# Beginning the first step of a chunked delta-rule scan beside the gates' projection that stands ahead of it

## The chip, the cores and the metric

The kernel runs on one core of one Trainium2 chip. The metric is the device time of one execution in microseconds; the table below gives the median of three runs and the one execution that the hardware profiler recorded.

## What is computed

The reference is two networks one after the other: a hybrid block of two layers, and a second block whose layers are a gated unit, an RWKV-7 layer, a latent attention and again a gated unit. The change lies in the RWKV-7 layer. Its features are projections of the modulated and shifted input `h`, and its scan is a delta rule over 16 heads of 64, once forward and once backward, first over the 256 tokens of the context and then over the 512 of the sequence:

```python
xs = h[:, :, None, :] + xx[:, :, None, :] * mu
rkvz = jnp.einsum('blcd,cde->blce', xs[:, :, :4], w_in)      # r, k, v, z
...
kk = (kk * lax.rsqrt(jnp.sum(kk * kk, axis=-1, keepdims=True) + 1e-12)).reshape(k.shape)
k_dir = k * (1 + (a - 1) * k_a)
...
def step(S, inp):
    s_kk = jnp.einsum('nbhvk,nbhk->nbhv', S, kk_t)
    S = S * w_t[..., None, :] - s_kk[..., :, None] * (kk_t * a_t)[..., None, :] + v_t[..., :, None] * k_t[..., None, :]
    y_t = jnp.einsum('nbhvk,nbhk->nbhv', S, inp[5]) if emit else None
...
return (out * jax.nn.silu(z)) @ w_out
```

The gates `z` are used only in the last line, after the scan.

## The kernel before

One stage of the program follows the other, and for each stage every engine has its own instruction stream, written out by hand: `features_*` makes r, k, v and z, `scan_*` runs the scan, `output_*` closes the layer. SP is the queue that loads, POOL the one that stores in the features. Matrices are kept with channels on the 128 partitions and the 768 tokens (256 + 512) in the columns.

**The features.** `features_pe_` makes four projections in the order r, k, v, z. Each is a wave (`wave_pe`) over m = 0 to 7, eight tiles of 128 output channels, and for each m there is one product of 256 and one of 512 columns (the two segments), of eight matmuls each. A matmul in 32-bit floats is two records in the profile. The products of one m go to PSUM banks 6 and 7, those of the next to 0 and 1, and ACT takes them out; banks 2 to 5 (`side`) are for small work which a wave calls behind each product by `beside(m, lo)`, where `lo` is 0 behind the first segment and 256 behind the second. For m = 0 and 7 the two segments are interleaved (line 1720). In the z wave (`behind_z`) the small work is one transpose of values behind m = 0. ACT puts the tiles through Silu (line 1984), and POOL stores them (line 2176). r, kk, the key products ka and kd and the log decays lw have been stored to device memory during the earlier waves; the scan loads them back tile by tile.

**The scan.** There are 12 steps, each a direction and a tile of 128 tokens, that is two chunks of 64. A step has three parts, each a generator on every engine:

- `chosen(s)`: PE sums the log decays in four pieces (`decays`, L2320, banks 0 to 3), ACT takes the exponentials of each piece (L2521, L2522), DVE multiplies them into kk and ka (L2623, L2626, the events `al` and `be`) and into kd and r. PE then forms the key products `L` (64 by 64 blocks, L333), ACT copies them with a sign (L2531, `nL`), and DVE inverts 16 by 16 blocks of them in a long row of small operations (L2642 to L2719), ACT scales the result (L2536), and DVE turns it (L2667, L2670, the event `out`).
- `solved(s)`: PE completes the inverse by block products (`blocks(0)`, `blocks(1)`, then a series), with masks by DVE (L2752) and POOL (L2846) between, and forms the products with the values.
- `carried(s)`: the state is taken through the two chunks.

`scan_slots` runs slots: in the slot that begins with s, PE and its partners interleave `chosen(s + 2)`, `solved(s + 1)` and `carried(s)` by a string of turns. The first slot (s = -2) therefore holds `chosen(0)` alone, the second (s = -1) `chosen(1)` and `solved(0)`.

**The border.** SP, ACT, DVE and POOL each begin the scan with waits on `ends(pl, "features") + stored(pl)`: on the last event of every engine in the features, and on the landing of every store, the gates' (`S_.z0`, `S_.z1`) among them. PE waits only for its operands. The scan's buffers lie in the arena `A` and over the ring of weight slabs `W` (rows of step 0, 1 and 2 and the keys of even steps in the ring), at addresses which the features' `h`, `xx`, `xs` and the slabs of the z wave use until the end.

Of the kernel before, what the change touches and what calls it, by code (L numbers as in the profile page):

```python
# [16 lines left out]
SC = 256  # L17
# [1852 lines left out]
def features_act(pl, e):  # L1870
# [124 lines left out]
def features_dve(pl, e):  # L1995
# [137 lines left out]
    end(pl, "features", "dve")  # L2133


def features_pool(pl, e):
# [40 lines left out]
    end(pl, "features", "pool")  # L2177


def stored(pl):  # L2180

    S_ = pl.S
    return [S_.lw0.at(10), S_.lw1.at(11), S_.r_out.at(7), S_.kk0_out.at(6), S_.kk1_out.at(7), S_.kd0_out.at(7),
            S_.kd1_out.at(7), S_.ka0_out.at(6), S_.ka0_out1.at(7), S_.ka1_out.at(6), S_.ka1_out1.at(7), S_.vt0.at(6),
            S_.vt1.at(7), S_.bon0.at(6), S_.bon1.at(7), S_.z0.at(6), S_.z1.at(7), S_.res.at("out")]

# [5 lines left out]


def lay_scan(pl):
    ring = pl.W[:, :, :].rearrange("p a b -> p (a b)")
    A, b = Arena(pl, beyond=2 * N), Place()
    b.AR = [ring[:, 2048 * i:2048 * i + 2048].rearrange("p (m a c) -> p m a c", m=8, a=2) for i in range(3)]
    keys = [ring[:, 6144:8192], A(2048)]  # L2200
    b.KA = [x[:, 0:1024].rearrange("p (m c) -> p m c", m=8) for x in keys]
    b.KD = [x[:, 1024:2048].rearrange("p (m c) -> p m c", m=8) for x in keys]
    b.LW, b.E, b.EM = A(1024), A(8, 2, P), A(8, P)
    b.VU = [A(1024) for _ in range(3)]
    b.GT = [A(16, 64) for _ in range(2)]
    b.RK = [[A(16, 64) for _ in range(2)] for _ in range(2)]
    b.KB = [[A(1024) for _ in range(2)] for _ in range(2)]
    b.nL, b.T16, b.Q16 = A(16, 64), A(16, 64), A(16, 64)
    b.nEt, b.nE, b.Z1, b.Z2 = A(16, 64), A(16, 64), A(16, 64), A(16, 64)
    b.Q = [A(16, 64) for _ in range(2)]  # L2210
    b.X, b.HB = A(1024), [A(8, P) for _ in range(2)]
    b.turned = A(1024)
    b.N, b.S = A(272), A(272)
    b.EL, b.EF, b.sc = A(4, 8), A(4, 8), A(8)
    return b


# [27 lines left out]
def scan_slots(pl, e, chosen, solved, carried, order):  # L2245


    for s in range(-2, SCAN_LAST):
        slots({"1": chosen(pl, e, s + 2) if s + 2 < SCAN_LAST else nothing(),
               "2": solved(pl, e, s + 1) if 0 <= s + 1 < SCAN_LAST else nothing(),  # L2250
               "c": carried(pl, e, s) if s >= 0 else nothing()}, order)


def scan_sp(pl, e):
# [11 lines left out]
    def decays(s):  # L2266
        n, tile = SCAN_STEPS[s]
        if s:
            e.wait_ge(*S_.decay_sums.at(s - 1, 3))
        e.dma_start(b.LW, pl.F[f"lw{n}"][tile]).then_inc(*S_.slw.next(s))  # L2270

    def keys(s):
        n, tile = SCAN_STEPS[s]
        if s >= 2:
            e.wait_ge(*S_.gram.at(s - 2, "last"))
        for name, dst, signal in ((f"ka{n}", b.KA[s % 2], (S_.ska0, S_.ska1)[s % 2]),
                                  (f"kd{n}", b.KD[s % 2], (S_.skd0, S_.skd1)[s % 2])):
            e.dma_start(dst, pl.F[name][tile].rearrange("p (m c) -> p m c", m=8)).then_inc(*signal.next(s))

    def rows(s):  # L2280
        n, tile = SCAN_STEPS[s]
        if s >= 3:
            e.wait_ge(*S_.carried.at(2 * (s - 3) + 1, "Y"))
        for name, a, signal in (("kk", 0, (S_.skk0, S_.skk1, S_.skk2)[s % 3]),
                                ("r", 1, (S_.sr0, S_.sr1, S_.sr2)[s % 3])):
            e.dma_start(b.AR[s % 3][:, :, a, :], pl.F[name][tile].rearrange("p (m c) -> p m c", m=8)).then_inc(
                *signal.next(s))

    for s in range(-3, SCAN_LAST):
# [16 lines left out]
    end(pl, "scan", "pe")  # L2306


def chosen_pe(pl, e, s):

    S_, b = pl.S, pl.scan
    n, _ = SCAN_STEPS[s]
    for j in range(4):
        at = ("decays", s, j)
        ps = take(pl, at, "0123")
        if j == 0:
            e.wait_ge(*S_.slw.at(s))
        e.wait_ge(*free(pl, at))
# [282 lines left out]

def scan_dve(pl, e):
    S_, b = pl.S, pl.scan
    for event in ends(pl, "features") + stored(pl):
        e.wait_ge(*event)
    e.memset(b.S, 0.0).then_inc(*S_.dve_wrote.next())
    e.wait_ge(*S_.dve_wrote.last())
    e.memset(b.S[:, 0:272:17], 1.0).then_inc(*S_.dve_wrote.next())
    e.memset(b.N, 0.0).then_inc(*S_.dve_wrote.next())
    e.wait_ge(*S_.dve_wrote.last())  # L2610
# [1263 lines left out]
```

## Time and profile before

| | us |
|---|---|
| median of three runs | 5358.34 |
| the three runs | 5358.34, 5347.9, 5358.88 |
| the profiled execution | 5337.04 |
| its span, first to last instruction | 5335.2 |
| PE busy in the span | 4952.2 |

The profiled execution has 1.84 us around its span, and it is 21.30 us shorter than the median of the runs. PE is busy in 93% of the span, DVE in 28% and ACT in 20%, so what matters is where PE has nothing to do. The border between the features and the scan lies at about 3097 us of the span.

### The profile page before, as it was taken

Reading aid. Unit: us, or ns where it says so; the run is one execution under the profiler, and the core shown is the slowest. Engines: PE = TensorE matmul, PEld = TensorE weight load, DVE = VectorE, ACT = ScalarE, POOL = GpSimd, SP = SyncE. Lnnn points to the kernel's source line nnn. Section 1 sums busy time; section 2 is a strip of 40 time slices with the busy share of each in tenths; the row PEclk is TensorE's granted clock in tenths of the full one; section 3 lists DMA queues with packets and bytes.
Section 4 is the critical chain, followed back from the end, with each engine's and each line's share of the span. In section 5 each row is a group of like instructions: output and inputs, shape, how many; then the busy total and the mean of one; then the engine's idle time right before and its main releaser. Section 6 shows DMA issues by size and latency. Waiting matters only on the chain.

```text
span 5335.2 us, 63185 instructions
## 1 busy us (share of the span) xinstructions
PE 4952.2 (93%) x27502; PEld 2753.1 (52%) x27502; DVE 1480.8 (28%) x2779; ACT 1074.7 (20%) x2066; POOL 323.9 (6%) x302
## 2 busy tenths in 40 slices
PE   7878999987899999999998978988899999989999
PEld 3444444444444444665454557877544555544444
DVE  1272120227222010110324146665311344410100
ACT  1121000012200012110214123433211333311210
POOL 0110000011000000000014100000000011000000
PEclk9879999987999999999999989999999999989999
DMA  3232212213212211111134222121311000101211
GB/s 114 84 123 78 79 67 75 73 72 126 87 71 74 71 53 63 49 52 41 63 128 134 102 84 72 52 71 28 119 54 53 22 26 27 41 25 70 87 71 55
DMA packets 91874, 378.39 MB, mean 71 GB/s; under 512 B 8144, under 2 KB 33744, under 8 KB 62160
## 3 DMA queue, kind: packets, MB, share of 16 engines
q1 hardware_dynamic: 78048, 327.44, 17.2%
q0 software_dynamic: 9808, 37.75, 2.1%
q10 hardware_dynamic: 3744, 9.14, 0.5%
q8 instruction: 220, 3.60, 0.3%
q14 instruction: 54, 0.44, 0.0%
HBM read 334.46 MB, written 39.85 MB: 70 GB/s over the span
## 4 chain that ended last, share of the span: by engine, by line
PE 69%; DVE 4%; ACT 2%; issue 2%; DMA 0%; POOL 0%; POOLq 0%; DVEq 0%; ACTq 0%; SPq 0%
PE ps L521 29%; PE ps L333 20%; PE ps L542 5%; PE ps L3265 2%; PE ps L1720 1%; PE ps L3192 1%; PE ps L339 1%; PE ps L3276 1%; PE ps L2370 1%; PE ps L3195 1%; PE ps L3191 1%; PE ps L921 1%; PE ps L3193 1%; PE ps L2320 0%; PE ps L1751 0%
## 5 line engine op out<-in xcount | busy, mean ns | idle before, releaser
L521 PE MATMUL ps<-A,W 128*128 128x512 f32 (+1 forms) x5408 | 2167.3, 561 | 23.4 <-DVE A L1643 6.2
L521 PEld LDWEIGHTS ps<-A,W 128*128 128x128 f32 x5408 | 1028.1, 191 | 1119.6 <-issue 1076.8
L333 PE MATMUL ps<-A,W 128*128 128x512 f32 (+3 forms) x2368 | 665.1, 445 | 13.7 <-DMA W<-in_rw_in 6.0
L333 PE MATMUL ps<-A 64*64 64x64 f32 (+3 forms) x8416 | 511.1, 242 | 114.1 <-ACT A L3418 23.1
L333 PEld LDWEIGHTS ps<-A 64*64 64x64 f32 (+2 forms) x8416 | 471.0, 153 | 223.5 <-issue 142.3
L333 PEld LDWEIGHTS ps<-A,W 128*128 128x128 f32 (+2 forms) x2368 | 352.9, 174 | 303.9 <-issue 273.3
L542 PE MATMUL ps<-W,A 128*128 128x512 f32 (+1 forms) x896 | 366.1, 572 | 1.8 <-ACT A L1507 1.8
L542 PEld LDWEIGHTS ps<-W,A 128*128 128x128 f32 x896 | 173.2, 194 | 192.9 <-issue 186.5
L435 ACT ACTIVATE A<-R 128x512 f32<-128x512 f32 (+1 forms) x96 | 52.6, 574 | 779.7 <-DVE R L1517 354.9
L1637 DVE SCALAR_TENSOR_TENSOR A<-ps,V,A 128x512 f32<-128x512 f32 (+1 forms) x48 | 31.0, 661 | 486.9 <-PE ps L333 486.3
L1517 DVE SCALAR_TENSOR_TENSOR R<-ps,MOD,R 128x512 f32<-128x512 f32 (+1 forms) x48 | 31.7, 662 | 439.8 <-PE ps L521 438.5
L339 PE MATMUL ps<-C,A 128*128 128x128 f32 x608 | 102.5, 295 | 46.6 <-DVE A L1187 46.4
L3409 ACT ACTIVATE A<-ps,A 128x256 f32<-128x256 f32 (+1 forms) x128 | 84.8, 667 | 293.9 <-DVE A L3530 293.9
L333 PE MATMUL ps<-W,A 64*64 64x64 f32 (+3 forms) x1856 | 137.7, 255 | 4.6 <-ACT A L2550 2.8
L1653 POOL TENSOR_TENSOR A<-A 128x1536 f32<-128x1536 f32 (+1 forms) x16 | 46.4, 2900 | 1526.6 <-ACT A L1610 1526.6
L339 PEld LDWEIGHTS ps<-C,A 128*128 128x128 f32 x608 | 71.7, 146 | 123.5 <-DVE A L1187 65.0
L333 PEld LDWEIGHTS ps<-W,A 64*64 64x64 f32 (+1 forms) x1856 | 119.6, 160 | 27.0 <-issue 22.2
L1610 ACT ACTIVATE A<-ps 128x256 f32<-128x256 f32 (+1 forms) x96 | 50.3, 526 | 369.9 <-PE ps L521 369.7
L1451 DVE TENSOR_TENSOR A<-A,ps 128x512 f32<-128x512 f32 x44 | 30.3, 689 | 334.0 <-PE ps L521 334.0
L3528 DVE TENSOR_REDUCE A<-ps 128x1 f32<-128x256 f32 (+1 forms) x128 | 71.4, 558 | 138.6 <-PE ps L3193 138.1
L1418 ACT ACTIVATE A<-ps 128x512 f32<-128x512 f32 x44 | 26.3, 597 | 369.3 <-PE ps L521 369.3
L2550 ACT ACTIVATE A<-ps 64x512 f32<-64x512 f32 x144 | 85.2, 591 | 62.2 <-PE ps L333 60.2
(353 smaller groups left out, 4238.1 us busy)
## 6 DMA issues: line engine op xcount, KB each, us to landing
W<-in_ada SPq DMA_DIRECT2D x48, 1024.0 KB, 5.4
W<-in_w_up SPq DMA_DIRECT2D x44, 1024.0 KB, 4.8
W<-in_w_down SPq DMA_DIRECT2D x32, 704.0 KB, 4.0
W<-in_w_in SPq DMA_DIRECT2D x18, 1024.0 KB, 4.8
W<-in_sgu_v SPq DMA_DIRECT2D x16, 1024.0 KB, 4.8
W<-in_sgu_u SPq DMA_DIRECT2D x16, 1024.0 KB, 4.7
W<-in_sgu_z SPq DMA_DIRECT2D x16, 1024.0 KB, 4.8
W<-in_sgu_o SPq DMA_DIRECT2D x16, 1024.0 KB, 4.8
```

The source lines that it names most:

```text
L333: r = e.matmul(out, a, b, start=start and i == 0, stop=stop and i == len(pairs) - 1, skip_group_check=loose)
L339: return e.transpose(out, in_, table(pl, "ident")[0:k, 0:k])
L521: t = e.matmul(ps, w[:, k, c:c + mc], x(k, seg), start=k == 0, stop=k == kt - 1)
L542: mm = e.matmul(ps, x(k0 + k, tile), w[:, k, :], start=k0 + k == 0, stop=k0 + k == kt - 1)
L921: t = e.matmul(ps[32 * k:32 * k + 32, :], b.cs[:, 4 * hf + k, :], w[:, k, :], start=hf == 0, stop=hf == 1)
L1720: t = e.matmul(y, w[:, k, :], b.x(k, s), start=k == 0, stop=k == 7)
L2370: e.matmul(by_heads(ps[c][HALF[c], :]), one[HALF[c], :], i, start=True, stop=False, skip_group_check=True)
L2550: e.activation(dst[HALF[c], 8 * g:8 * g + 8, :], by_heads(bank(pl, at)[HALF[c], :]), ACT.Copy).then_inc(*S_.act_blocks.next((s, g, stage), ...
L3191: e.matmul(ps[0][:, 0:SC], qn, kh[:, 0:SC], start=True, stop=False)
L3265: t = e.matmul(ps[:, :], uq[j][:, k, 0:P], b.cq[:, k, :], start=k == 0, stop=k == 5)
L3409: e.activation(b.pr[:, z, lo:hi], bank(pl, at)[:, 0:hi - lo], ACT.Exp, bias=m[:, 2:3], scale=b.rq[:, p % 2, 2 * i + j:2 * i + j + 1], accu ...
L3528: e.tensor_reduce(m[:, part:part + 1], bank(pl, at)[:, 0:w], AX, ALU.max).then_inc(*made.next())
```

## The change

The first step's `chosen(0)` is taken out of the scan and given to the features, beside the z wave, and the scan begins with the slot s = -1. The buffers are laid anew so that everything that `chosen(0)` touches lies in the first 11,880 columns of the arena, where only `h` and `xx` were, which the last interpolation of the z wave (`lerped.at(3, 7)`) is the last to read; what lay in the ring for step 0 is in the arena, and the masked products `GT` are in the ring. SP loads step 0 and the decays of step 1 behind the z wave's slabs. At the start of the scan POOL waits for all stores as before; SP, ACT and DVE no longer wait for those of the gates.

```diff
@@ features_sp @@
             slab_load(pl, e, ("rw_in", c, m), ins["rw_in"][c, m])
+    first_step_sp(pl, e)
@@ features_pe_ @@
+    first = chosen_pe(pl, e, 0, side)
+
     def behind_z(m, lo):
         if m == 0 and not lo:
             turn(7)
+        for _ in range({1: 4, 2: 1}.get(m, 0) if lo else 0):
+            next(first)
@@ features_act @@
+    first = chosen_act(pl, e, 0)
     for m in range(8):
         for s in segs:
...
                 *S_.act_projected.next(at, frees=at))
+            for _ in range({(1, SC): 4, (3, 0): 1, (5, 0): 1}.get((m, s[0]), 0)):
+                next(first)
@@ features_dve @@
+    first_step_dve(pl, e)
     end(pl, "features", "dve")
+
+
+def first_step_dve(pl, e):
+    S_, x = pl.S, pl.scan
+    e.wait_ge(*S_.lerped.last())
+    for event in keys_stored(pl):
+        e.wait_ge(*event)
+    e.memset(x.S, 0.0).then_inc(*S_.dve_wrote.next())
...
+    for _ in chosen_dve(pl, e, 0):
+        pass
@@ lay_scan @@
-    b.AR = [ring[:, 2048 * i:2048 * i + 2048].rearrange("p (m a c) -> p m a c", m=8, a=2) for i in range(3)]
-    keys = [ring[:, 6144:8192], A(2048)]
+    rows = [A(2048), ring[:, 0:2048], ring[:, 2048:4096]]
+    keys = [A(2048), ring[:, 4096:6144]]
+    b.AR = [x.rearrange("p (m a c) -> p m a c", m=8, a=2) for x in rows]
...
+    b.GT = [ring[:, 6144 + 1024 * i:7168 + 1024 * i].rearrange("p (h c) -> p h c", h=16) for i in range(2)]
@@ scan_slots @@
-    for s in range(-2, SCAN_LAST):
+    for s in range(-1, SCAN_LAST):
@@ new @@
+def first_step_sp(pl, e):
+
+    e.wait_ge(*pl.S.lerped.at(3, 7))
+    for event in keys_stored(pl):
+        e.wait_ge(*event)
+    decays_sp(pl, e, 0)
+    keys_sp(pl, e, 0)
+    rows_sp(pl, e, 0)
+    decays_sp(pl, e, 1)
@@ scan_sp @@
-    for event in ends(pl, "features") + stored(pl):
+    for event in ends(pl, "features") + keys_stored(pl) + values_stored(pl):
@@ chosen_pe @@
-        ps = take(pl, at, "0123")
+        ps = take(pl, at, ring)
@@ scan_act, scan_dve @@
-    for event in ends(pl, "features") + stored(pl):
+    for event in ends(pl, "features") + values_stored(pl):
@@ scan_pool @@
-    for event in ends(pl, "features") + stored(pl):
+    for event in ends(pl, "features") + keys_stored(pl) + values_stored(pl) + [S_.z0.at(6), S_.z1.at(7)]:
```

The order on PE at the border, before: behind the last pair of the z wave (L1720) come the four pieces of step 0's decays (L2320), the key products of step 0, two pieces of step 1's decays, and then `blocks(0)` of step 0. A matmul is one row here.

```order
L1720 MATMUL ps1<-A,W 128x512
L2320 MATMUL ps0<-C,A 128x256 [waits act_projected,slw]
...
L2320 MATMUL ps3<-C,A 128x256 [waits value_copied]
L2320 MATMUL ps3<-C,A 128x256
L333 MATMUL ps0<-W 64x64 [waits decayed,dve_operands]
L333 MATMUL ps1<-W 64x64
...
L2320 MATMUL ps2<-C,A 128x256 [waits decayed,slw]
L2320 MATMUL ps2<-C,A 128x256
L2320 MATMUL ps3<-C,A 128x256 [waits decayed]
L2320 MATMUL ps3<-C,A 128x256
L333 MATMUL ps0<-A 64x64 [waits act_blocks,decayed,blocks_solved]
```

PE has this whole row of work between its last z product and `blocks(0)`. The same engine and place of the changed kernel, where the decays have line 2368:

```order
L1721 MATMUL ps1<-A,W 128x512
L2368 MATMUL ps0<-C,A 128x256 [waits act_projected,slw]
L2368 MATMUL ps0<-C,A 128x256
L2368 MATMUL ps1<-C,A 128x256 [waits act_projected]
L2368 MATMUL ps1<-C,A 128x256
L333 MATMUL ps2<-A 64x64 [waits act_blocks,decayed,blocks_solved]
```

Step 0's pieces and key products are gone from here, and step 1's two pieces are now in banks 0 and 1, which the last tiles of the z wave hold until ACT has taken them out. `blocks(0)` takes banks 2, 3, 0 and 1.

In the z wave of the changed kernel, PE behind m = 1 and m = 2:

```order
L333 MATMUL ps1<-A,W 128x512 x7
L2368 MATMUL ps2<-C,A 128x256 [waits value_copied,slw]
...
L2368 MATMUL ps5<-C,A 128x256 [waits value_copied]
L2368 MATMUL ps5<-C,A 128x256
L333 MATMUL ps6<-A,W 128x256 [waits act_projected,slab0]
L333 MATMUL ps6<-A,W 128x256 x7
L333 MATMUL ps7<-A,W 128x512 [waits act_projected]
L333 MATMUL ps7<-A,W 128x512 x7
L333 MATMUL ps2<-A 64x64 [waits decayed,dve_operands]
```

The eight matmuls of the decays stand between m = 1 and m = 2, and the 32 of the key products, of which the last row is the first, between m = 2 and m = 3; before, these products followed one another with nothing between.

On ACT in the changed kernel the exponentials stand between the tiles of m = 1 and m = 2:

```order
L2569 ACT_TABLE_LOAD
L2569 ACTIVATE A<-ps2 128x512 [waits decay_sums]
L2570 ACTIVATE A<-ps2 128x256
L2569 ACTIVATE A<-ps3 128x512 [waits decay_sums]
L2570 ACTIVATE A<-ps3 128x256
...
L1990 ACT_TABLE_LOAD [waits z0]
L1990 ACTIVATE A<-ps6 128x256 [waits projected]
```

There are two table loads more than before on ACT, both here, and the one at the start of the scan stays.

## Rows read from the trace of the kernel before

**Rows 1.** The page: span, and busy time of each engine.
```profile
span 5335.2 us, 63185 instructions
PE 4952.2 (93%) x27502; PEld 2753.1 (52%) x27502; DVE 1480.8 (28%) x2779; ACT 1074.7 (20%) x2066; POOL 323.9 (6%) x302
```

**Rows 2.** Chain of work from 3013 to 3140 us: start, us, what.
```profile
3024.81 61.96 PE ps L333 x192
...
3098.29 2.59 DMA g_z<-A
...
3101.02 3.62 DMA A<-f_lw
...
3117.01 1.98 DVE A L2642 x2
...
3131.58 1.76 DVE A L2667 x2
```

**Rows 3.** PE in order of time, 3084 to 3165 us: start, us, instructions, idle before.
```profile
3086.59 10.49 PE L1720 MATMUL ps<-A,W 128*128 128x256 f32 x32
3104.69 5.98 PE L2320 MATMUL ps<-C,A 128*128 128x256 f32 x16 [7.61 <-DMA A<-f_lw]
3113.85 1.98 PE L333 MATMUL ps<-W 64*64 64x64 f32 x64 [3.19 <-DVE A L2627]
...
3133.43 3.52 PE L333 MATMUL ps<-A 64*64 64x64 f32 x64 [13.88 <-DVE A L2667]
3137.72 1.99 PE L2320 MATMUL ps<-C,A 128*128 128x256 f32 x8 [0.78 <-DVE A L2752]
3140.77 2.10 PE L333 MATMUL ps<-A 64*64 64x64 f32 x64 [1.05 <-ACT A L2522]
...
3150.01 1.10 PE L333 MATMUL ps<-A,W 64*64 64x64 f32 x62
```

**Rows 4.** Windows: length, busy time and count by engine, PEclk, DMA share, GB/s.
```profile
3013.00:3097.00 84.00, 83.42 (x262) 48.93 (x262) 8.93 (x11) 7.09 (x15) 5.84 (x10) 1.00 0.15 58
3112.00:3133.00 21.00, 5.69 (x72) 4.35 (x72) 17.80 (x33) 4.30 (x10) 0.00 (x0) 0.60 0.46 135
3137.00:3165.00 28.00, 19.14 (x452) 15.46 (x453) 21.63 (x40) 11.72 (x23) 2.19 (x2) 0.98 0.09 30
3165.00:3640.00 475.00, 426.04 (x9135) 377.10 (x9134) 306.40 (x509) 183.10 (x350) 19.62 (x18) 0.96 0.23 66
```

**Rows 5.** ACT in order of time, 3097 to 3112 us.
```profile
3097.12 0.87 ACT L1984 ACTIVATE A<-ps 128x256 f32<-128x256 f32 x2 [9.73 <-PE ps L1720]
3106.87 1.28 ACT L2521 ACT_TABLE_LOAD   x1 [8.88 <-PE ps L2320]
3108.16 0.60 ACT L2521 ACTIVATE A<-ps 128x512 f32<-128x512 f32 x1
...
3109.39 0.41 ACT L2522 ACTIVATE A<-ps 128x256 f32<-128x256 f32 x1
```

**Rows 6.** DVE in order of time, 3111 to 3147 us.
```profile
3112.53 1.22 DVE L2626 TENSOR_TENSOR W<-W,A 128x1024 f32<-128x1024 f32 x1
...
3136.98 2.85 DVE L2752 TENSOR_TENSOR A<-ps,C 64x512 f32<-64x512 f32 x4 [3.66 <-PE ps L333]
3142.91 2.85 DVE L2752 TENSOR_TENSOR A<-ps,C 64x512 f32<-64x512 f32 x4 [3.07 <-PE ps L333]
3145.79 1.23 DVE L2623 TENSOR_TENSOR W<-W,A 128x1024 f32<-128x1024 f32 x1
```

**Rows 7.** POOL in order of time, 3095 to 3150 us.
```profile
3101.10 1.84 POOL L2830 MEMSET A<- 128x1024 f32 x2 [2.27 <-DMA g_z<-A]
3138.48 1.09 POOL L2846 TENSOR_TENSOR A<-A,C 128x512 f32<-128x512 f32 x1 [35.54 <-DVE A L2752]
```

**Rows 8.** DMA issues, 3095 to 3130 us: count, KB each, us from issue to landing.
```profile
W<-f_kk SPq DMA_DIRECT2D x2, 512.0 KB, 7.2
W<-f_r SPq DMA_DIRECT2D x2, 512.0 KB, 8.8
```

More of the change, by code:

```diff
@@ L2132, in features_dve @@
                 *S_.value_copied.next((m, s[0]), frees=at))
+    first_step_dve(pl, e)
     end(pl, "features", "dve")
+def first_step_dve(pl, e):
[4 more added lines that the diff above has]
+    e.memset(x.S, 0.0).then_inc(*S_.dve_wrote.next())
+    e.wait_ge(*S_.dve_wrote.last())
+    e.memset(x.S[:, 0:272:17], 1.0).then_inc(*S_.dve_wrote.next())
+    e.memset(x.N, 0.0).then_inc(*S_.dve_wrote.next())
+    e.wait_ge(*S_.dve_wrote.last())
+    for _ in chosen_dve(pl, e, 0):
+        pass
 def features_pool(pl, e):
@@ L2177, in features_pool, with keys_stored, values_stored @@
     end(pl, "features", "pool")
-def stored(pl):
+def keys_stored(pl):
     S_ = pl.S
     return [S_.lw0.at(10), S_.lw1.at(11), S_.r_out.at(7), S_.kk0_out.at(6), S_.kk1_out.at(7), S_.kd0_out.at(7),
-            S_.kd1_out.at(7), S_.ka0_out.at(6), S_.ka0_out1.at(7), S_.ka1_out.at(6), S_.ka1_out1.at(7), S_.vt0.at(6),
-            S_.vt1.at(7), S_.bon0.at(6), S_.bon1.at(7), S_.z0.at(6), S_.z1.at(7), S_.res.at("out")]
+            S_.kd1_out.at(7), S_.ka0_out.at(6), S_.ka0_out1.at(7), S_.ka1_out.at(6), S_.ka1_out1.at(7)]
+def values_stored(pl):
+    S_ = pl.S
+    return [S_.vt0.at(6), S_.vt1.at(7), S_.bon0.at(6), S_.bon1.at(7), S_.res.at("out")]
 SCAN_ORDER = ([0, 1, 2, 3, 4, 5], [1, 0, 5, 4, 3, 2])
@@ L2198, in lay_scan @@
     A, b = Arena(pl, beyond=2 * N), Place()
-    b.AR = [ring[:, 2048 * i:2048 * i + 2048].rearrange("p (m a c) -> p m a c", m=8, a=2) for i in range(3)]
-    keys = [ring[:, 6144:8192], A(2048)]
+    rows = [A(2048), ring[:, 0:2048], ring[:, 2048:4096]]
+    keys = [A(2048), ring[:, 4096:6144]]
+    b.AR = [x.rearrange("p (m a c) -> p m a c", m=8, a=2) for x in rows]
     b.KA = [x[:, 0:1024].rearrange("p (m c) -> p m c", m=8) for x in keys]
     b.KD = [x[:, 1024:2048].rearrange("p (m c) -> p m c", m=8) for x in keys]
+    b.GT = [ring[:, 6144 + 1024 * i:7168 + 1024 * i].rearrange("p (h c) -> p h c", h=16) for i in range(2)]
     b.LW, b.E, b.EM = A(1024), A(8, 2, P), A(8, P)
+    b.nL, b.T16, b.Q16 = A(16, 64), A(16, 64), A(16, 64)
+    b.N, b.S = A(272), A(272)
+    b.EL, b.EF, b.sc = A(4, 8), A(4, 8), A(8)
     b.VU = [A(1024) for _ in range(3)]
-    b.GT = [A(16, 64) for _ in range(2)]
     b.RK = [[A(16, 64) for _ in range(2)] for _ in range(2)]
-    b.KB = [[A(1024) for _ in range(2)] for _ in range(2)]
-    b.nL, b.T16, b.Q16 = A(16, 64), A(16, 64), A(16, 64)
-    b.nEt, b.nE, b.Z1, b.Z2 = A(16, 64), A(16, 64), A(16, 64), A(16, 64)
     b.Q = [A(16, 64) for _ in range(2)]
     b.X, b.HB = A(1024), [A(8, P) for _ in range(2)]
+    b.KB = [[A(1024) for _ in range(2)] for _ in range(2)]
     b.turned = A(1024)
-    b.N, b.S = A(272), A(272)
-    b.EL, b.EF, b.sc = A(4, 8), A(4, 8), A(8)
+    b.nEt, b.nE, b.Z1, b.Z2 = A(16, 64), A(16, 64), A(16, 64), A(16, 64)
     return b
@@ L2251, in scan_slots, with decays_sp, keys_sp, rows_sp @@
                "c": carried(pl, e, s) if s >= 0 else nothing()}, order)
+def decays_sp(pl, e, s):
+    S_, b = pl.S, pl.scan
+    n, tile = SCAN_STEPS[s]
+    if s:
+        e.wait_ge(*S_.decay_sums.at(s - 1, 3))
+    e.dma_start(b.LW, pl.F[f"lw{n}"][tile]).then_inc(*S_.slw.next(s))
+def keys_sp(pl, e, s):
+    S_, b = pl.S, pl.scan
+    n, tile = SCAN_STEPS[s]
+    if s >= 2:
+        e.wait_ge(*S_.gram.at(s - 2, "last"))
+    for name, dst, signal in ((f"ka{n}", b.KA[s % 2], (S_.ska0, S_.ska1)[s % 2]),
+                              (f"kd{n}", b.KD[s % 2], (S_.skd0, S_.skd1)[s % 2])):
+        e.dma_start(dst, pl.F[name][tile].rearrange("p (m c) -> p m c", m=8)).then_inc(*signal.next(s))
+def rows_sp(pl, e, s):
+    S_, b = pl.S, pl.scan
+    n, tile = SCAN_STEPS[s]
+    if s >= 3:
+        e.wait_ge(*S_.carried.at(2 * (s - 3) + 1, "Y"))
+    for name, a, signal in (("kk", 0, (S_.skk0, S_.skk1, S_.skk2)[s % 3]),
+                            ("r", 1, (S_.sr0, S_.sr1, S_.sr2)[s % 3])):
+        e.dma_start(b.AR[s % 3][:, :, a, :], pl.F[name][tile].rearrange("p (m c) -> p m c", m=8)).then_inc(
+            *signal.next(s))
+def first_step_sp(pl, e):
[6 more added lines that the diff above has]
+    decays_sp(pl, e, 1)
 def scan_sp(pl, e):
     S_, b = pl.S, pl.scan
-    for event in ends(pl, "features") + stored(pl):
+    for event in ends(pl, "features") + keys_stored(pl) + values_stored(pl):
         e.wait_ge(*event)
@@ L2264, in values @@
             *(S_.sv0, S_.sv1, S_.sv2)[u % 3].next(u))
[L2266 to L2289, printed above, removed]
+    for s in range(-2, SCAN_LAST):
         if 0 <= s + 1 < SCAN_LAST:
             values(2 * s + 2)
-        if s + 3 < SCAN_LAST:
-            decays(s + 3)
+        if 1 < s + 3 < SCAN_LAST:
+            decays_sp(pl, e, s + 3)
         if 0 <= s + 1 < SCAN_LAST:
@@ L2296, in scan_sp @@
         if s + 3 < SCAN_LAST:
-            keys(s + 3)
-            rows(s + 3)
+            keys_sp(pl, e, s + 3)
+            rows_sp(pl, e, s + 3)
 def scan_pe(pl, e):
@@ L2306, in scan_pe, with chosen_pe @@
     end(pl, "scan", "pe")
-def chosen_pe(pl, e, s):
+def chosen_pe(pl, e, s, ring="0123"):
     S_, b = pl.S, pl.scan
@@ L2324, in chosen_pe @@
     at = [("L", s, par) for par in range(2)]
-    ps = [take(pl, x, "0123") for x in at]
+    ps = [take(pl, x, ring) for x in at]
     e.wait_ge(*S_.dve_operands.at(s, "al"))
@@ L2603, in scan_dve @@
     S_, b = pl.S, pl.scan
-    for event in ends(pl, "features") + stored(pl):
+    for event in ends(pl, "features") + values_stored(pl):
         e.wait_ge(*event)
[L2606 to L2610, printed above, removed]
     scan_slots(pl, e, chosen_dve, solved_dve, carried_dve, "2 2 1 1 c 1 1 1 1 1 1 1 2 1 2 2 c".replace(" ", ""))
@@ L2826, in scan_pool @@
     S_, b = pl.S, pl.scan
-    for event in ends(pl, "features") + stored(pl):
+    for event in ends(pl, "features") + keys_stored(pl) + values_stored(pl) + [S_.z0.at(6), S_.z1.at(7)]:
         e.wait_ge(*event)
```

## The prediction

> **What bounds the kernel now.** I read the page first: PE is busy in 4952.2 of 5335.2 us [rows 1], so a change of this kind can win only where PE stands idle or slow. The chain of waits shows the place. It runs through PE's z wave up to 3097.08 us (3086.59 + 10.49 [rows 3]), and then leaves PE: the store of the last gates lands (2.59 us), the log decays of step 0 are loaded (3.62), PE sums them, ACT and DVE work, PE makes the key products, and from 3117.01 to 3133.34 it is nearly all DVE, with ACT once between [rows 2]. Only at 3133.43 does PE begin `blocks(0)` of step 0, after 13.88 us in which it waited for DVE [rows 3]. From the last z product to `blocks(0)` are 36.35 us, and PE has work in about 11.7 of them (5.98 + 1.98 + two pieces of step 1's decays, which hide in the gap). The windows show the second loss: the granted clock, 1.00 during the z wave, averages 0.60 from 3112 to 3133 and is 0.98 in the slot after [rows 4]; it is the lower of the two levels, 1.2 GHz, for most of the gap, which PE entered after 7.61 us without work [rows 3].
>
> **What the change removes.** Everything between 3097.08 and 3133.43 goes from the path: the wait for the last gates' store, the load of the decays, step 0's sums and exponentials, its operands, the key products, and the 16.3 us of inverse blocks. These are run beside the z wave, where DVE, after its last interpolations and value copies, and ACT are nearly idle: 8.93 and 7.09 us of 84 [rows 4].
>
> **What it puts into the z wave.** PE is the bound there (83.42 of 84 us, and the six tiles m = 1 to 6 follow one another in 61.96, 10.33 each [rows 2, 4]), so all its added work counts in full.
> - The decays of step 0 are 16 records of 128x256. At full clock 8 of them take 1.99 us with their tail [rows 3], so 3.98 is the upper bound; the z wave's own pace gives the lower: 61.96 us over 96 records of 256 and 96 of 512 columns is 0.215 for a 256, or 3.44. I take 3.7.
> - The key products are 64 records of 64x64. Step 1's, at full clock, are 62 in 1.10 and two more just before [rows 3]; I take 1.2. The 1.98 at 3113.85 was at the low clock and is the upper end.
> - Sum 4.9 (4.6 to 6.0); the z wave ends at 3102.0.
>
> Does PE wait in the wave? Behind m = 1 (about 3035.0, that is 3024.8 + 10.3) the sums take 3.7. ACT takes a table load of 1.28 and four pairs of exponentials, two of which took 1.64 (3108.16 to 3109.80 [rows 5]), and is through by about 3041; DVE's `al` and `be`, 1.2 each [rows 6], are ready by 3043.5. PE comes to the key products at 3038.7 + 10.3 = 3049.0: 5.5 us of cover. If that cover were gone, each us late would stop the z products queued behind. The loads of step 0 are issued at about 3020, when the last interpolation is done, and even the slowest landing, 8.8 us for r [rows 8], is in before its use. ACT's two added table loads (2.6 us) delay Silu tiles, but a bank is wanted again only two tiles, 20 us, later. DVE's inverse (16.3 us from 3055) ends by 3080, the scaling on ACT behind m = 5 included, 20 us before it is needed. SP stands in the wait for step 0's sums, with only step 1's decays behind it; POOL issues the gates' stores as before. All of this I cost at nothing.
>
> **What stays on the path behind the wave.** `blocks(0)` needs four banks, and two of them now hold step 1's pieces, which before were made and taken out in the gap. So, from 3102.0: ACT takes the tile out of bank 0 and PE begins the first piece, 0.6 us (the two tiles took 0.87 [rows 5]); four records at 0.23 and the hand-over to ACT, 1.3 (before, at half clock, 2.18 from 3104.69 to 3106.87 [rows 3, 5]); the table load 1.28; two pairs of exponentials 1.64; and back to PE 0.15. `blocks(0)` begins at 3102.0 + 5.0 = 3107.0, against 3133.43: **26.4 us** earlier.
>
> It also begins at full clock. Before, DVE could begin the first mask 3.55 us after its start (3136.98), while for `blocks(1)`, the same 64 products at full clock, it was 2.14 (3140.77 to 3142.91) [rows 3, 6]. That gives **1.4 us** more if PE keeps its clock over about 3.5 us with little work.
>
> The ScalarE: Activation LUTs page of the Trainium skill (What ACT_TABLE_LOAD costs) speaks against part of this: a switch to another set costs about 1.28 us and a drain of about 1.38, and one switch stands on the path. The trace shows the next activation at 3108.16, right after the load's 1.28 us [rows 5], with no drain behind it; by the page's price the gain would be 1.4 us less than by my sum.
>
> **Does something else come late?** SP issues the keys and rows of step 1 only after ACT's last z tile, at about 3103.1, where before they were on their way 22 us ahead of `blocks(0)`. Four issues take about 2 us, and the slowest landing 8.8 [rows 8], so they are in by 3114. DVE wants kk of step 1 12.36 us after `blocks(0)` began (3145.79 [rows 3, 6]), less 1.4 for the clock: at 3118.0. The cover is 4 us, and thin. POOL still waits for the last gates' store: 3103.2 + 2.6, then the two memsets of 1.84 [rows 7], by 3108; its first add is wanted 1.5 us behind the first mask (3138.48 against 3136.98 [rows 6, 7]), at 3110.6. The rest of the scan (3165 to 3640, PE 426 of 475 us [rows 4]) has the same order with buffers at other addresses and banks turned by two; nothing in it starts at a fixed time, so it shifts as a whole.
>
> **Sum.** 26.4 + 1.4 = 27.8 us, bounds 22 (blocks at low clock, dearer inserted work, the exponentials late by 2) to 30 (inserted work at its lower bound, no wait for bank 0). Span 5335.2 - 27.8 = 5307.4, and with the 1.8 us around it the profiled execution would be 5309.2. The median of the runs shown is 21.3 us above the profiled execution; against it the forecast is 5358.34 - 27.8 = 5330.5. Between a profile at 5337.04 and runs up to 5358.88 some 10 us either way come from the runs, not from the change. What a measurement of this kernel can tell from no change is about 0.2%, 10.7 us.
>
> **Rivals.**
> - *The clock falls in the slot after* (chance 0.09). PE is busy in only 19.14 of 28 us there [rows 4], and the scan as a whole ran at 0.96. For: the clock did fall after the 7.61 us idle. Against: before, this slot kept 0.98. Half of its 19 us of work at half speed costs 10: 5340.
> - *Step 1's rows, or the operands in the wave, come late* (0.05). It decides once four transfers need more than 4 us beyond the slowest seen. At 10 us of wait the time is 5340.
> - *The change doesn't bring forward what ends the scan* (0.04): a later slot waits for something that starts when it did before, and gives the gain back. I find no such wait in the rows; 5358.
> - *Slower* (0.04). A wave that PE ran without a gap gets two short pieces of other work, one of them 64x64 products. If the clock fell there and did not come back until the wave's end, the five tiles behind, 51.6 us, would take twice as long: 5330.5 + 51.6 = 5382. It turns the result once the low clock holds for 28 us. Against: the z wave, transposes and all, shows 1.00 [rows 4], and the added work leaves no idle time.
>
> **How the numbers follow.** The forecast has 0.78, with a range of its own of 5318 to 5342 (the bounds of the sum and the scatter of the runs). The first two rivals lie at its upper end. I give 5314 to 5346, which leaves out the last two and the tails. Faster by over 0.2%: 0.78 + 0.09 + most of 0.05, 0.91; within 0.2%: 0.05; slower: 0.04.
>
> **What the changed profile should show.** PE has no wait above 0.5 us in the z wave, which ends 4.6 to 6.0 us later. The granted clock is 1.00 across the border. A table load on ACT stands right behind the first piece of step 1. `blocks(0)` starts 9.5 to 11 us behind the old end of the wave and takes 2.1 us, not 3.5. DVE's long row of small operations lies between 3055 and 3080. After that each slot is as long as it was. I am wrong if PE waits for the key products' operands, if DVE in the slot after waits for kk of step 1, or if the clock falls.

## The result: 0.67% faster by the first runs, 0.34% by all of them

| | kernel before | changed kernel |
|---|---|---|
| first session, median (5 runs each) | 5358.34 | 5316.88 |
| ratio there, 95% interval | | 0.9933, 0.9917 to 0.995 |
| profiled execution | 5337.04 | 5318.4 |
| its span | 5335.2 | 5316.6 |
| all runs of all sessions: mean (count) | 5344.5 (88) | 5326.2 (29) |

Over all runs the difference of the means is 18.4 us with a standard error of 2.7; single runs of the kernel before lie between 5319 and 5373 us. The first session's medians of five lay 13.8 us above and 9.3 us below these means, so its difference of 41.5 us is 23 us too large. I therefore read the change where it acts, in the traces. In the rows, `[1.80 <-DVE ...]` means that the engine stood idle for 1.80 us, until DVE had finished. I cut each span in three: the **head**, up to the start of the z wave's first product; the **border**, from there to DVE's first mask of step 0; the **tail**, the rest.

PE of the changed kernel, in order of time from 3005 to 3160 us, answers to [rows 3]:

```profile
3022.13 10.57 PE L1721 MATMUL ps<-A,W 128*128 128x256 f32 x32 [1.80 <-DVE A L2054]
...
3043.52 3.61 PE L2368 MATMUL ps<-C,A 128*128 128x256 f32 x16
3046.97 10.48 PE L333 MATMUL ps<-A,W 128*128 128x256 f32 x32
3057.39 1.16 PE L333 MATMUL ps<-A 64*64 64x64 f32 x64
...
3099.88 10.49 PE L1721 MATMUL ps<-A,W 128*128 128x256 f32 x32
3110.94 1.97 PE L2368 MATMUL ps<-C,A 128*128 128x256 f32 x8 [0.56 <-ACT A L1990]
3115.37 2.10 PE L333 MATMUL ps<-A 64*64 64x64 f32 x64 [2.47 <-ACT A L2570]
3118.35 1.99 PE L2368 MATMUL ps<-C,A 128*128 128x256 f32 x8 [0.88 <-DVE A L2795]
```

Step 0's sums (3.61) and key products (1.16) stand in the wave with no wait; the wave takes 88.24 us (3022.13 to 3110.37), against 83.50 before (3013.58 to 3097.08). `blocks(0)` starts 5.00 us behind it and takes 2.10, at full clock. The start of the wave is 8.55 us later than before, though nothing ahead of it was changed; other runs of both kernels put it elsewhere again (table below).

ACT and DVE of the same kernel, in order of time; they answer to [rows 5] and [rows 6]:

```profile
3112.30 1.28 ACT L2569 ACT_TABLE_LOAD   x1 [1.01 <-PE ps L2368]
3113.59 0.60 ACT L2569 ACTIVATE A<-ps 128x512 f32<-128x512 f32 x1
```

```profile
3048.61 1.23 DVE L2666 TENSOR_TENSOR A<-A 128x1024 f32<-128x1024 f32 x1 [13.80 <-ACT A L2569]
3049.75 1.22 DVE L2669 TENSOR_TENSOR A<-A 128x1024 f32<-128x1024 f32 x1
...
3063.63 1.97 DVE L2685 STREAM_TRANSPOSE A<-A 128x512 f32<-128x512 f32 x2 [10.25 <-ACT A L2579]
...
3086.66 1.90 DVE L2710 STREAM_TRANSPOSE A<-A 128x512 f32<-128x512 f32 x2
3117.61 2.85 DVE L2795 TENSOR_TENSOR A<-ps,C 64x512 f32<-64x512 f32 x4 [29.06 <-PE ps L333]
```

The key products' operands are ready at 3050.97, 6.4 us before PE wants them; the inverse lies between 3063 and 3089, beside the wave. The first mask is at 3117.61: the border is 95.48 us, before 3136.98 - 3013.58 = 123.40. **The border gained 27.9 us.** The tails are 2198.2 us before and 2199.0 after, and with the head's 8.55 that is the difference of the two spans, 18.6.

The windows around it (columns as in [rows 4], the granted clock third from the end) show the clock kept from the wave's end through `blocks(0)`:

```profile
3110.40:3115.40 5.00, 1.99 (x10) 1.49 (x11) 0.00 (x0) 3.79 (x7) 0.54 (x1) 1.00 0.54 172
3115.40:3145.00 29.60, 20.61 (x504) 16.77 (x504) 21.36 (x39) 11.11 (x22) 4.01 (x4) 0.95 0.33 93
```

What the second window lacks is lost at the slot's end: the clock is 1.00 up to 3139, and 0.73 from 3139 to 3145, where PE waits 4.58 us for ACT's scaling. The kernel before has the same wait (4.57).

### The profile page after: what moved, and what is told of

Same layout as the page of the kernel before. It is cut to its first block, busy times and chain, and to the rows that moved or that the text cites. A ratio compares the mean times of both kernels' runs of the same rounds, so it can differ in the third digit from the quotient of the medians.

```text
span 5316.6 us, 63186 instructions
## 1 busy us (share of the span) xinstructions
PE 4958.3 (93%) x27502; PEld 2757.2 (52%) x27502; DVE 1480.1 (28%) x2779; ACT 1077.2 (20%) x2068; POOL 323.9 (6%) x302
## 4 chain that ended last, share of the span: by engine, by line
PE 70%; DVE 4%; ACT 2%; issue 2%; DMA 0%; POOL 0%; POOLq 0%; DVEq 0%; ACTq 0%
PE ps L521 29%; PE ps L333 20%; PE ps L542 5%; PE ps L3308 2%; PE ps L1721 2%; PE ps L3235 1%; PE ps L339 1%; PE ps L3319 1%; PE ps L2418 1%; PE ps L3238 1%; PE ps L3234 1%; PE ps L921 1%; PE ps L3236 1%; PE ps L1752 0%; PE ps L2977 0%
## 5 line engine op out<-in xcount | busy, mean ns | idle before, releaser
L333 PE MATMUL ps<-A,W 64*64 64x64 f32 (+3 forms) x3264 | 711.1, 386 | 44.7 <-DVE R L2859 13.5
L333 PEld LDWEIGHTS ps<-A,W 128*128 128x128 f32 (+2 forms) x3264 | 397.6, 167 | 338.7 <-issue 308.9
L333 PE MATMUL ps<-A 64*64 64x64 f32 (+3 forms) x8416 | 498.7, 243 | 72.6 <-ACT A L3461 23.1
L333 PEld LDWEIGHTS ps<-A 64*64 64x64 f32 (+2 forms) x8416 | 458.0, 153 | 179.3 <-issue 96.3
L333 PE MATMUL ps<-W,A 64*64 64x64 f32 (+3 forms) x1472 | 118.6, 261 | 2.1 <-ACT A L2598 1.9
L333 PEld LDWEIGHTS ps<-W,A 64*64 64x64 f32 (+1 forms) x1472 | 102.5, 164 | 22.6 <-issue 17.9
L2795 DVE TENSOR_TENSOR A<-ps,C 64x512 f32<-64x512 f32 x96 | 66.1, 689 | 136.0 <-PE ps L333 133.7
```

The lines of the kernel that those rows point to most:

```text
L333: r = e.matmul(out, a, b, start=start and i == 0, stop=stop and i == len(pairs) - 1, skip_group_check=loose)
L2795: e.tensor_tensor(dst[HALF[c], 8 * g:8 * g + 8, :], by_heads(bank(pl, at)[HALF[c], :]), masked_by(pl, mask, HALF[c], 8), ALU.mult).then_in ...
```

## The experiments

All parts in us, each row from one profiled execution; x4_early, x5_zwaits, x8_filler and x10_early_filled were executed only this once, and nothing is read from their whole time. *Release* is when PE starts after ACT's scaling of step 1, counted from the start of the z wave; the tail begins at the first mask.

| kernel | head | z wave | border | release | tail |
|---|---|---|---|---|---|
| before | 3013.6 | 83.50 | 123.40 | 150.8 | 2198.2 |
| x11_before | 3010.0 | 83.49 | 122.71 | 150.1 | 2195.3 |
| changed | 3022.1 | 88.24 | 95.48 | 122.9 | 2199.0 |
| x0_again | 3040.1 | 88.24 | 95.48 | 122.9 | 2209.3 |
| x12_third | 3032.0 | 88.25 | 95.48 | 122.9 | 2202.3 |
| x1_waits | 3013.1 | 83.49 | 119.78 | 147.2 | 2202.1 |
| x2_loads | 3031.5 | 83.49 | 115.33 | 142.8 | 2202.8 |
| x3_sums | 3039.3 | 86.95 | 109.96 | 137.4 | 2211.9 |
| x4_early | 3016.0 | 94.63 | 101.87 | 129.3 | 2199.2 |
| x5_zwaits | 3031.5 | 88.24 | 99.08 | 126.5 | 2209.3 |
| x7_next | 3016.1 | 91.69 | 95.20 | 125.8 | 2209.1 |
| x9_filled | 3031.6 | 91.69 | 95.20 | 121.8 | 2199.1 |
| x10_early_filled | 3013.5 | 92.25 | 99.49 | 126.9 | 2201.8 |
| x8_filler | 3028.0 | 83.50 | 122.54 | 150.0 | 2202.4 |

The border of the changed kernel repeats (95.48 three times), that of the kernel before to 0.7 us (123.40 and 122.71). Heads, the same code in all, move by 30 us, and tails, nearly the same code, by 17.

### The same kernels again: x0_again, x11_before, x12_third

No edit.

> The changed kernel once more. I split each profile in three: the head up to the first product of the z wave (before 3013.6 us, changed 3022.1), the border from there to DVE's first mask of step 0 (before 123.4, changed 95.5), and the tail from there to the end of the span (before 2198.2, changed 2199.0). Theory path: the change is worth the border's 27.9 us and nothing else; head and tail vary from run to run with the granted clock, in both kernels. Then the border is 95.5 within 0.3 again, the tail is within 8 us of 2199, and the medians of the two kernels lie 20 to 36 us apart. Rival, more than the border: the medians differed by 41.5 us because the slots after run better as well; then the tail comes out shorter than 2190, or the medians are again 40 us apart.

> The changed kernel a third time, to settle what the runs of the first two left open: its medians were 41.5 us below the kernel before in one session and 8.6 in the other, with single runs scattered over 37 us, while the border measured 95.48 us both times. Theory path: border 95.5 again, head and tail anywhere in 3013 to 3040 and 2198 to 2212; set against the mean granted clock of each run, the two kernels' runs lie on two parallel lines, about 17 us apart at equal clock (the kernel before has some 12 us of clock loss in its own border, which this comparison hides). Rival: the change has a cost in the rest of the program; then the lines are not parallel or lie less than 12 us apart.

> The kernel before, unchanged, as a kernel of its own. Theory path: border 123.4 within 0.3; its head is anywhere in 3013 to 3040 us like that of the changed kernel, so that the 3013.6 of the first profile was one draw; its median differs from that of the other runs of the same kernel by up to 10 us for no reason in the code. Rival: head and tail of the kernel before are shorter than those of the changed one as a rule: head under 3018 again.

Ratios to the kernel before: x0_again 0.9974 (0.9954 to 0.9995), x12_third 0.9959 (0.994 to 0.9978), x11_before 0.9988 (0.9968 to 1.0007). The borders of the changed kernel came as expected. That of x11_before, 122.71, lies 0.7 below the first and missed "within 0.3": behind the same wait of 3.19 us its key products ran at full clock, in 1.16 us, where the first profile has 1.98 [rows 3]. Its head, 3010.0, is under 3018 again, which was the rival's sign; x8_filler, the kernel before with fillers behind this place, has 3028.0, and x1_waits, x4_early and x10_early_filled, with the changed layout, have 3013 to 3016. So a low head is no mark of the kernel before. The medians of x0_again, only 8.6 us apart, missed "20 to 36", and its tail missed "within 8 us" by 2. Each run lists its mean granted clock, and against it both kernels lie on lines: 4.12 us for each 0.001 of clock before (83 runs), 4.28 after (29), with 2.0 and 2.3 us left over. At a clock of 0.953 they stand at 5343.3 and 5325.3, parallel within the scatter and 18.0 us apart, as x12_third's expectation had it (17). So nearly all scatter of the runs goes with the granted clock.

### The change in steps: x1_waits, x2_loads, x3_sums

x1_waits, against the changed kernel (x2_loads leaves `first_step_sp` in the features):

```diff
@@ features_sp, features_pe_, features_act, features_dve @@
-    first_step_sp(pl, e)
...
-        for _ in range({1: 4, 2: 1}.get(m, 0) if lo else 0):
-            next(first)
...
-    first_step_dve(pl, e)
@@ scan_slots, scan_sp, scan_dve @@
-    for s in range(-1, SCAN_LAST):
+    for s in range(-2, SCAN_LAST):
...
+    first_step_sp(pl, e)
...
+    first_step_dve(pl, e)
```

> The changed kernel's layout and its fewer waits, with all work and loads of step 0 back at the start of the scan. Theory path: SP no longer waits for the landing of the last gates (3.0 us), all else is as before: border 123.4 - 3.0 = 120.4 (119.9 to 121.0). Rival, that fewer waits alone make much of the gain: border under 115.

> As x1_waits, with the loads of step 0 issued during the z wave as in the changed kernel; its work still stands in the scan. Theory path: PE begins the sums 0.6 us behind the z wave, where before it was 7.6; its idle is then too short for the clock to fall, which gives 0.9 on the first sum and 0.8 on the key products; blocks(0) still starts at the low clock behind DVE's inverse. Border 123.4 - 7.0 - 1.7 = 114.7 (114 to 117).

x3_sums keeps the sums and what follows from them in the wave:

```diff
-        for _ in range({1: 4, 2: 1}.get(m, 0) if lo else 0):
+        for _ in range({1: 4}.get(m, 0) if lo else 0):
...
```

> As the changed kernel, but only the sums, exponentials and operands of step 0 stand beside the z wave; key products and inverse are in the scan. Theory path: the z wave is 3.6 us longer, then 1.4 for the key products, 1.1 for their copy, 16.4 for the inverse, and 3.5 for a slow blocks(0): border 83.5 + 3.6 + 18.9 + 3.5 = 109.5 (108.5 to 111). The inverse's 16 us on DVE would then be the larger half of the whole gain. Rival, that PE's work in the wave is dearer than its busy time: z wave longer than 88 us.

Borders of 119.78, 115.33 and 109.96 against 120.4, 114.7 and 109.5. Fewer waits gave 3.6 us, early loads 4.5, sums and exponentials beside the wave 5.4, key products and inverse 14.5. Against x11_before the first step is 2.9 us, and 3.0 were expected. x1_waits fell 0.1 below its stated span because the clock was back when the key products came; PE there, in order of time:

```profile
3101.68 5.41 PE L2358 MATMUL ps<-C,A 128*128 128x256 f32 x16 [5.12 <-DMA A<-f_lw]
3110.38 1.16 PE L333 MATMUL ps<-A 64*64 64x64 f32 x64 [3.30 <-DVE A L2661]
```

Their 1.16 us stands against 1.98 in [rows 3], in the kernel before at the low clock. x2_loads is within its span, but not by the way expected: its sums did run at full clock, its key products, behind a longer wait, did not. PE of x2_loads, in order of time:

```profile
3115.55 3.69 PE L2358 MATMUL ps<-C,A 128*128 128x256 f32 x16 [0.56 <-ACT A L1985]
3123.50 1.99 PE L333 MATMUL ps<-A 64*64 64x64 f32 x64 [4.25 <-DVE A L2661]
```

As whole-kernel medians the steps are invisible: 5353, 5340 and 5353 against 5342.6. Set against the clock as above they show: moved along the line to a clock of 0.953, the means of the ten runs each are 5341.7, 5336.3 and 5333.4, in order between 5343.3 and 5325.3. These differences are smaller than the border's, because a comparison at equal clock leaves out what a change gains in clock.

### The waits put back: x5_zwaits

```diff
@@ scan_act, scan_dve; the same two waits are added in scan_sp @@
-    for event in ends(pl, "features") + values_stored(pl):
+    for event in ends(pl, "features") + values_stored(pl) + [pl.S.z0.at(6), pl.S.z1.at(7)]:
```

> The changed kernel with SP's, ACT's and DVE's waits for the gates' stores put back. Theory path: the last store lands some 3 to 5.6 us after its issue at 3111.6 in the changed profile, and ACT may take the first exponential of step 1 only then, not at 3112.3: blocks(0) and the border 2.3 to 5 us later, 98 to 100.5. Rival: these waits are hidden behind PE's first two sums, border 95.5 to 96.

The border is 99.08: 3.6 us dearer, as expected. `blocks(0)` starts 2.2 us later, and the longer wait costs the clock too, another 1.4. PE of x5_zwaits, in order of time:

```profile
3120.26 1.97 PE L2368 MATMUL ps<-C,A 128*128 128x256 f32 x8 [0.56 <-ACT A L1990]
3126.89 3.51 PE L333 MATMUL ps<-A 64*64 64x64 f32 x64 [4.66 <-ACT A L2570]
```

### The cover in the wave: x4_early and x10_early_filled

```diff
-        for _ in range({1: 4, 2: 1}.get(m, 0) if lo else 0):
+        for _ in range({1: 5}.get(m, 0) if lo else 0):
             next(first)
```

> The changed kernel with the key products of step 0 directly behind the sums, ahead of the z products of m = 2. Theory path: PE reaches them at the sums' end, but al and be are ready only 3.9 us later (in the changed profile the sums end at 3047.1 and be at 3050.97), and all z products queue behind: z wave 88.2 + 3.9 = 92.1 us, border 99.4 (98.8 to 100.2). This prices the cover that the chosen place gives. Rival, the clock: an idle PE of 4 us inside the wave brings the low clock and the next products run at half pace; z wave over 94 us.

x10_early_filled puts eight products between:

```diff
+            filler(pl, e, 6, 8)
             next(first)
...
+def filler(pl, e, bank_no, n):
+    e.wait_ge(*pl.bank_freed.get(pl.occupant[bank_no], pl.S.const.last()))
+    for _ in range(n):
+        e.matmul(pl.banks[bank_no][:, 0:256], table(pl, "ident"), pl.C[:, 0:256], start=True, stop=True)
```

> As x4_early, with eight products of 128x256 on constants into a free bank ahead of the key products, in the 3.94 us in which PE waited for their operands. Theory path: x4_early's z wave of 94.6 us was 88.2 + 3.9 of wait + 2.5 of low clock; with the fillers the clock stays, and the wave takes 92.1 (91.9 to 92.4). Rival, that the 2.5 us were something else than the clock: 94.6 again.

x4_early's wave took 94.63 us: the wait is the expected 3.94, and 2.45 more went to the clock. Over 94 us was the rival's sign. Windows of x4_early, columns as in [rows 4]; PEclk is the third number from the end:

```profile
3041.00:3043.00 2.00, 0.02 (x1) 0.00 (x0) 0.50 (x1) 1.98 (x6) 0.00 (x0) 1.00 0.49 104
3043.00:3045.00 2.00, 0.04 (x4) 0.07 (x5) 2.00 (x5) 0.98 (x1) 0.00 (x0) 0.56 0.41 162
3047.00:3049.00 2.00, 2.00 (x5) 1.64 (x6) 0.27 (x1) 0.00 (x0) 0.00 (x0) 0.50 0.00 0
3049.00:3051.00 2.00, 2.00 (x8) 1.62 (x8) 0.00 (x0) 0.00 (x0) 0.00 (x0) 0.74 0.00 0
```

With the fillers PE waited 0.49 us and the wave took 92.25, as the clock reading demands (PE of x10_early_filled):

```profile
3038.34 3.62 PE L2278 MATMUL ps<-C 128*128 128x256 f32 x16
3042.44 1.16 PE L333 MATMUL ps<-A 64*64 64x64 f32 x64 [0.49 <-DVE A L2679]
```

### Step 1's sums in the wave too: x7_next and x9_filled

`begun_pe` is `chosen_pe(pl, e, 1, side)`, and ACT has the same; the slot s = -1 passes over the four turns that this takes from it.

```diff
+        if m == 4 and lo:
+            for _ in range(4):
+                next(pl.begun_pe)
...
@@ scan_pool @@
...
+    for _ in solved_pool(pl, e, 0):
+        pass
+    for event in [S_.z0.at(6), S_.z1.at(7)]:
+        e.wait_ge(*event)
```

> The changed kernel with all four sums and exponentials of step 1 in the z wave too, behind m = 4, and POOL making its first two adds before it waits for the gates' stores. Theory path: the z wave is 3.6 us longer; blocks(0) follows it after 1.0 us (two tiles to take out) and not 5.0; blocks(1) no longer waits for exponentials, 0.9. Border to the first mask 95.5 + 3.6 - 4.0 = 95.1, and 1.3 us in all by the second group of masks (5.9 us behind the first in the changed kernel, 5.0 here). Rival: ACT's two further table loads or PE's added work make the wave longer than that and nothing is won; border 96.5 or more.

x9_filled adds, behind `blocks(0)` of step 0, `filler(pl, e, 7, 6)`.

> As x7_next, with six products of 128x256 columns on constants into a free bank between step 0's first and second block products, whose result nobody uses. In x7_next PE idled 3.1 us there and the clock was at its lower level for the next 10 us: the second masks came 101.5 us behind the start of the z wave (changed kernel 101.4), and PE's first product behind step 1's scaling 125.8 (changed kernel 122.9). Theory path: the fillers keep the clock; first mask 95.2, second 100.3 (100.0 to 100.6), step 1's scaling released at 121 (120 to 122), so 1 to 3 us better than the changed kernel. Rival: what is late in x7_next is not PE's pace but the order; 125 to 126 again.

x7_next: first mask 95.20 as computed, but the second masks at 101.48, where 100.1 was expected, and the release 2.9 us later than in the changed kernel. The runs' median was 5322.55 against 5340.09, ratio 0.9974 (0.9954 to 0.9995). PE idled in the slot, and its products ran slowly. PE of x7_next, in order of time:

```profile
3109.05 2.10 PE L333 MATMUL ps<-A 64*64 64x64 f32 x64 [1.27 <-ACT A L1995]
3114.28 3.24 PE L333 MATMUL ps<-A 64*64 64x64 f32 x64 [3.13 <-DVE A L2809]
3119.11 3.68 PE L333 MATMUL ps<-C,A 128*64 128x128 f32 x32 [1.59 <-DVE A L2809]
```

The same places of x9_filled, with the fillers in the idle time:

```profile
3126.59 2.86 PE L2283 MATMUL ps<-C 128*128 128x256 f32 x12
3129.78 2.10 PE L333 MATMUL ps<-A 64*64 64x64 f32 x64 [0.34 <-DVE A L2817]
3133.48 1.97 PE L333 MATMUL ps<-C,A 128*64 128x128 f32 x32 [1.59 <-DVE A L2817]
```

Second masks at 100.33, release at 121.8: 1.1 us better than the changed kernel and 4.0 better than x7_next, which differs only by useless products. By release x9_filled is the best version made here: median 5315.66 (6 runs) against 5344.72 for the kernel before in its session, ratio 0.994 (0.992 to 0.996). That it beats the changed kernel rests on its trace; 1.1 us does not show in medians.

### A filler in the kernel before: x8_filler

```diff
+    if s == 0:
+        e.wait_ge(*pl.bank_freed.get(pl.occupant[5], pl.S.const.last()))
+        for i in range(26):
+            e.matmul(pl.banks[5][:, 0:256], table(pl, "ident"), pl.C[:, 0:256],
+                     start=True, stop=True)
```

> The kernel before, with 26 products of 128x256 columns on constants into a free bank, on PE ahead of step 0's first block products; nobody uses their result. They keep PE busy while DVE inverts. Theory path: the clock is back at full when blocks(0) starts, so the first mask comes 2.2 us behind its start and not 3.55: border 123.4 - 1.4 = 122.0 (121.8 to 122.3, or 122.5 if the fillers end late). Rival: the slow blocks(0) is not a matter of the clock but of the first use after a wait; border stays 123.4.

Inconclusive. The fillers took 11.4 us and ended 4.54 us early; `blocks(0)` still took 3.46. PE of x8_filler, in order of time:

```profile
3131.12 11.38 PE L2349 MATMUL ps<-C 128*128 128x256 f32 x52
3147.05 3.46 PE L333 MATMUL ps<-A 64*64 64x64 f32 x64 [4.54 <-DVE A L2673]
```

The border of 122.54 is that of x11_before (122.71), whose key products also ran at full clock; the fillers themselves gave at most 0.2 us. x9_filled and x10_early_filled decided the question.

## Why the prediction was right, and what it left out

**The path.** The bound (36.35 us from the wave's end to `blocks(0)`) was read rightly, and the steps x1 to x3 show that it came off in the parts named: waits, loads, exponentials, and as the largest part key products and inverse.

**The inserted work.** Estimated 4.9 us, measured 4.74 (3.61 + 1.16, less what overlaps).

**Behind the wave.** Estimated 5.0 us from its end to `blocks(0)`, measured 5.00. The table load took 1.28 us and the exponential followed 0.01 later. The page ScalarE: Activation LUTs of the Trainium skill (What ACT_TABLE_LOAD costs) has a drain of 1.38 us besides; this trace doesn't show one on the path.

**The clock.** Estimated 1.4 us; `blocks(0)` now leads to its first mask in 2.24 us, not 3.55, so 1.3. The rival that the clock falls in the next slot did not come true here (1.00 up to 3139), but it did in x7_next and x5_zwaits, at 1.4 to 4 us: right as a mechanism, and near.

**Late arrivals.** DVE took up kk of step 1 104.3 us behind the wave's start, as estimated (104.4), 6.8 us after its landing. POOL was mis-sized: I had its memsets done 2.6 us before its first add is wanted. The last gates' store now lands beside step 1's loads, 5.5 us after its issue and not 2.6, and the cover is 0.03 us. POOL of the changed kernel, which answers to [rows 7]:

```profile
3111.57 0.54 POOL L2199 DMA_DIRECT2D g_z<-A  x1 [10.07 <-ACT A L1990]
3117.24 1.84 POOL L2873 MEMSET A<- 128x1024 f32 x2 [5.12 <-DMA g_z<-A]
3119.11 1.08 POOL L2889 TENSOR_TENSOR A<-A,C 128x512 f32<-128x512 f32 x1
```

**The sum.** 27.8 us foreseen, 27.9 in the border (27.2 against x11_before). The bounds of 22 and 30 are wider than the terms named for them, which come to 23.3 and 28.7; and the rival *Slower* counted 28 us of low clock where it needs 28 us of full-clock work at half pace, some 56 us by the clock.

**What was luck.** The measured 5316.88 is inside the stated range, but 13.6 us below the forecast of 5330.5 and 1.1 below the forecast's own range of 5318 to 5342. The first session's 41.5 us owe as much to which five runs were drawn as to the change: over all runs the gain is 18.4 us, and that is 9.4 below the sum and below its lower bound of 22. So the mechanism of the border was right, and one term was not: that everything behind it "shifts as a whole", at no cost.

**What the sum lacked, and what stays open.** The mean over all runs moved by 18.4 us (13 to 24), not 27.9. From the windows, the kernel before loses 0.33 of 36.3 us and 0.06 of 31.0 to the low clock in its border, 13.8 us; the changed kernel 0.05 of 29.6, 1.5. That should raise the mean clock of a run by 12.3 / 5335 = 0.0023, to 0.9551. It is 0.9528 in both. At 4.12 us for 0.001 those 0.0023 are 9.5 us, just what is missing: outside the border the changed kernel's runs had less clock, by more than chance easily gives (the standard errors of the two mean clocks are 0.0003 and 0.0006). One place is seen. A stretch that ends the latent attention, between two table loads of ACT (4634.53 and 4858.62 us in the kernel before), takes 224.1 us in the kernel before, x11_before and x8_filler, 227.9 in the changed kernel's first trace, and 231.5 to 232.2 in the ten others. In both kernels the clock dips and comes back in its first 45 us; it then stays up to 72 us behind the stretch's start in the kernel before, but falls again at 48 in x12_third. The same 60 us of it, from 19 us behind its start, in the kernel before and then in x12_third, windows of 20:

```profile
4653.38:4673.38 20.00, 16.23 (x94) 11.78 (x91) 11.18 (x27) 5.37 (x15) 0.00 (x0) 0.91 0.31 128
4673.38:4693.38 20.00, 13.58 (x68) 8.69 (x68) 6.48 (x18) 5.73 (x16) 0.00 (x0) 0.91 0.00 1
4693.38:4713.38 20.00, 13.50 (x64) 7.60 (x62) 6.64 (x17) 5.59 (x16) 0.00 (x0) 0.91 0.00 0
```

```profile
4640.70:4660.70 20.00, 16.21 (x94) 11.87 (x91) 11.18 (x27) 5.39 (x15) 0.00 (x0) 0.91 0.30 125
4660.70:4680.70 20.00, 14.06 (x52) 8.61 (x52) 5.53 (x16) 5.30 (x16) 0.00 (x0) 0.74 0.00 0
4680.70:4700.70 20.00, 15.42 (x52) 9.77 (x52) 4.96 (x13) 3.94 (x12) 0.00 (x0) 0.66 0.01 1
```

The code there is the same. PE waits 2.5 us for each group of exponentials, in both kernels and at both levels of the clock, and a group takes 7.3 us at the full clock and 10.2 at the low one. Added up in windows of 3 us, the stretch loses 18.2 us to the low clock in the kernel before, x11_before and x8_filler, 20.5 in the changed kernel's first trace, and 25.6 in x0_again, x12_third, x1_waits and x5_zwaits. The 7.4 us between are just what the stretch takes longer; they are most of the missing 9.5, and 0.0014 of the missing 0.0023 in the mean clock of a run. The three traces of the old layout and the eleven of the new part cleanly here. x1_waits is among the eleven, with no work of step 0 in the wave, and so is x5_zwaits, with the waits put back: it needs neither the early work nor the dropped waits. What the eleven share is the new layout of the buffers and the rewritten loads. By what path those move a clock 1,500 us later, no run here tells.

## What to carry to other kernels

Where one stage ends in a chain on other engines before the matrix engine can begin the next, the head of that chain belongs beside the stage ahead; what has to be made room for is its buffers, and the price is the matrix engine's own busy time. Place each inserted product only after its operands are sure to be there: 3.9 us too early cost 6.4. And when the gain is half a per cent, measure the stage in the trace from a fixed instruction to a fixed instruction, and set each run against its mean granted clock, before believing a median of five. Then ask for the difference between the stage and the whole: here a third of what the stage gained was gone from the whole.

## What the hardware showed that I had not expected

A wait on the matrix engine can cost more than itself: 3.94 us without products cost 6.39, 3.13 us in x7_next put the next 10 us of products at half pace, and in both cases products that compute nothing, put into the wait, won the clock back (2.4 and 4.0 us). In x8_filler, where they ended 4.54 us before the work they were to help, they did not. Waits of 2.47, 1.27 and 0.49 us in these places did not have that effect. The length of a wait alone doesn't settle it: 3.19 us ahead of the key products went with 1.98 us of products in the kernel before and with 1.16 in x11_before, the same program. And a scatter of 54 us between runs of one kernel follows the granted clock to within 2 us.
